# The last part of w_out: row by row through all six gated rows, instead of the first two rows begun on five of them

## What is computed

```
def swiglu(x, w_in, w_out):
    a, b = jnp.split(x @ w_in, 2, axis=-1)
    return (jax.nn.silu(a) * b) @ w_out
...
    for l in range(DEPTH):
        h = h + 0.5 * swiglu(rmsnorm(h, ffn1_norm[l]), ffn1_w_in[l], ffn1_w_out[l])
        u = rmsnorm(h, mix_norm[l])
        ...
        y_c = mem_attention(q_c, rmsnorm(mem, mem_norm[l]), w_mem_kv[l])
        ...
        h = h + 0.5 * swiglu(rmsnorm(h, ffn2_norm[l]), ffn2_w_in[l], ffn2_w_out[l])
    return rmsnorm(h, final_norm)
```

## Time and profile before

| | us |
|---|---|
| median of 3 runs | 2153.34 (2151.99 to 2153.64) |
| the profiled execution | 2153.76 |
| its span in the trace | 2151.7 |
| TensorE busy | 2109.1 (98% of the span) |
| VectorE busy | 1605.8 (75%) |
| GpSimd busy | 1483.6 (69%) |
| ScalarE busy | 1112.0 (52%) |
| chain that ended last: TensorE, VectorE, ScalarE | 92%, 4%, 2% |

### The profile page before, as it was taken

The page is one execution under the profiler, slowest core; times in us unless marked ns, Lnnn a source line. Parts: engine busy times, 40 slices in busy tenths (PEclk is TensorE's granted clock), DMA queues, the critical chain, the costliest instruction groups (busy, mean ns, idle before and its releaser), DMA issues.

```text
span 2151.7 us, 39307 instructions
## 1 busy us (share of the span) xinstructions
PE 2109.1 (98%) x13990; PEld 1917.8 (89%) x13990; DVE 1605.8 (75%) x2860; ACT 1112.0 (52%) x2203; POOL 1483.6 (69%) x1110
## 2 busy tenths in 40 slices
PE   9999998999999999999999999989999999999997
PEld 6999996878888889999889999978888888999996
DVE  6888887468764578888768888765787555888884
ACT  5656653454553356565356565435445533656652
POOL 6888876644445678787778888765444366888874
PEclk9999999999999999999999999999999999999999
DMA  5333333322222323333334333332222133233332
GB/s 171 115 119 103 113 117 113 109 69 69 66 63 85 105 86 105 111 99 105 103 94 133 101 102 125 113 125 85 69 66 73 55 104 97 90 108 99 115 98 83
DMA packets 95234, 213.16 MB, mean 99 GB/s; under 512 B 10401, under 2 KB 13641, under 8 KB 94793
## 3 DMA queue, kind: packets, MB, share of 16 engines
q1 hardware_dynamic: 90864, 205.42, 30.5%
q10 hardware_dynamic: 4184, 5.31, 0.7%
HBM read 208.58 MB, written 3.68 MB: 99 GB/s over the span
## 4 chain that ended last, share of the span: by engine, by line
PE 92%; DVE 4%; ACT 2%; issue 1%; DMA 0%; ACTq 0%; DVEq 0%; SPq 0%
PE banks_two L1082 9%; PE banks_two L1083 9%; PE banks_two L1084 9%; PE bank L1084 7%; PE bank L1083 7%; PE bank L1082 7%; PE bank L950 6%; PE bank L951 6%; PE bank L952 6%; PE banks_two L950 5%; PE banks_two L951 4%; PE banks_two L952 4%; PE tbank L1315 1%; DVE yL L2193 1%; PE bank L1146 1%
## 5 line engine op out<-in xcount | busy, mean ns | idle before, releaser
L806 POOL TENSOR_SCALAR wH<-raw 128x1024 fp32r<-128x1024 f32 (+2 forms) x184 | 173.4, 942 | 416.6 <-PE bank L952 211.2
L809 POOL TENSOR_TENSOR wL<-raw,wH 128x1024 fp32r<-128x1024 f32 (+2 forms) x184 | 389.3, 2116 | 15.4
L851 POOL TENSOR_TENSOR wL<-wS,wH 128x512 fp32r<-128x512 f32 x208 | 268.9, 1301 | 41.9 <-ACT wH L1531 38.4
L851 POOL TENSOR_TENSOR wL<-raw,wH 128x512 fp32r<-128x512 f32 x208 | 267.3, 1301 | 11.6 <-ACT wH L1537 8.0
L1082 PE MATMUL banks_two<-u1H,wH 128*128 128x256 f32 x864 | 244.9, 283 | 3.4 <-DVE far4L L2073 3.4
L1083 PE MATMUL banks_two<-u1H,wL 128*128 128x256 f32 x864 | 244.5, 283 | 0.0
L1084 PE MATMUL banks_two<-u1L,wH 128*128 128x256 f32 x864 | 244.5, 283 | 0.0
L1537 ACT ACTIVATE wH<-raw 128x512 fp32r<-128x512 f32 x208 | 130.5, 630 | 181.1 <-PE bank L1084 181.1
L857 POOL TENSOR_TENSOR wS<-raw 128x512 f32<-128x512 f32 x104 | 135.1, 1299 | 82.7 <-issue 60.6
L950 PE MATMUL bank<-u1H,wH 128*128 128x512 f32 x480 | 191.1, 398 | 0.0
L951 PE MATMUL bank<-u1H,wL 128*128 128x512 f32 x480 | 187.5, 391 | 0.0
(11 more groups left out here) (413 smaller groups left out, 7190.2 us busy)
## 6 DMA issues: line engine op xcount, KB each, us to landing
raw<-in_wA SPq DMA_DIRECT2D x296, 256.0 KB, 3.0
raw<-in_wM SPq DMA_DIRECT2D x96, 512.0 KB, 3.5
raw<-in_wO SPq DMA_DIRECT2D x128, 256.0 KB, 2.9
raw<-in_wA SPq DMA_DIRECT2D x28, 512.0 KB, 3.5
raw<-in_wC SPq DMA_DIRECT2D x32, 384.0 KB, 3.0
raw<-in_wR SPq DMA_DIRECT2D x32, 256.0 KB, 2.6
keep<-in_memT SPq DMA_DIRECT2D x4, 512.0 KB, 5.2
mem<-in_memT SPq DMA_DIRECT2D x2, 1024.0 KB, 5.8
```

What stands on the lines that cost most here:

```text
L806: pool.tensor_scalar(wH[:, w, 0:cols], raw[:, slot, 0:cols], 1.0, 0.0, ALU.mult, ALU.add).then_inc(rounded, 1)
L809: pool.tensor_tensor(wL[:, w, 0:cols], raw[:, slot, 0:cols], wH[:, w, 0:cols].bitcast(F32), ALU.subtract).then_inc(split_done, 1)
L851: pool.tensor_tensor(half_slot(wL_flat, n), full, half_slot(wH_flat, n).bitcast(F32), ALU.subtract).then_inc(pool_low, 1)
```

## The change

Rows 0 and 1 are treated as rows 2 to 7: each output row runs over all six gated rows in turn, and then the next begins. No instruction is added or removed.

```
                             take_unit(u + i)
-                            if i < 2:
-                                rows(i, range(N_OUT - 1))
-                            else:
-                                rows(i, range(N_OUT)).then_inc(unit_used, 1)
-                            if i == 1:
-                                for first in range(2):
-                                    rows(first, (N_OUT - 1,)).then_inc(unit_used, 1)
+                            rows(i, range(N_OUT)).then_inc(unit_used, 1)
```

## The result

| | before | after |
|---|---|---|
| median of 5 runs, us | 2153.34 (2151.99 to 2153.64) | 2163.24 (2160.99 to 2164.11) |
| ratio, 95% interval | | 1.0045 (1.0031 to 1.0060) |
| profiled execution / span | 2153.76 / 2151.7 | 2161.78 / 2159.8 |

The change makes the kernel 9.9 us slower. The forecast was 4.6 slower, and 2163.24 lies above its range.

What follows compares the result with a forecast made beforehand. TensorE, busy 98% of the span, was taken to bound the kernel. Part 2 adds 2 x 2.25 and part 1 2 x 0.05, 4.6 us on the median of 2153.34: 2157.9 us, range 2155.6 to 2160.6.

Steps and rivals of the forecast that it cites:

- The new wait: Row 0's last gated row, both parts and layers: TensorE stands still about 2.15 us, 2.25 with the restart.
- Part 2 reaches the end whole: Feed-forward part 2 of each layer: the 2.25 us delay goes fully to the end, 4.5 us for both.
- Where it is covered: part 1 of each layer: Before the memory projection: VectorE's chain sets its start, so the standstill costs only 0.05 us per layer.
- 9.12 us for the memory's low parts: Part 1, VectorE's chain between output rows 3 and 4: 9.12 us listed for making the memory's low parts.
- isn't waited for in either case: Part 2: GpSimd gets row 0's slot earlier and row 1's later, and nothing waits for it.
- TensorE's own delay of about 2 us shortens its standstill of 7.49 to some 5.5: Memory projection after part 1: TensorE arrives about 2 us later, so its wait falls from 7.49 to some 5.5 us.
- I leave the clock at full: TensorE at the new 2.15 us standstills: no clock fall, as an earlier fall took about 4 us.
- the rival: TensorE's clock falls in all four new standstills, 1.5 us each, row 1 also later: 10.6 us, 2163.9; 4%.
- Both slow rivals: Part 1 not covered, all four standstills count: 9.0 us, 2162.3, 6%; clock falls in the standstills: 10.6, 2163.9, 4%.
- Row 0 handed over sooner: VectorE begins row 0 some 1.1 us sooner in part 1; finishing it earlier brings nothing in part 2.

Runs made afterwards that it cites:

- filled: The change plus nine unread matmuls in each of the four standstills, against the kernel before: 2161.65 us, 1.0040.
- held kernels: Five kernels, old, new or mixed row order, where GpSimd delays weight splits until VectorE's subtractions finish: 2140.21, 2149.77, 2148.01, 2140.35, 2139.51 us against some 2153 before.
- part 2 alone: Row by row order only in feed-forward part 2 of both layers, against the kernel before: 2160.99 us, 1.0036.
- part 1 alone: Row by row order only in feed-forward part 1 of both layers, against the kernel before: 2157.82 us, 1.0020.
- after held: The change, with GpSimd's splits from the third memory slot on waiting for VectorE's subtractions, against the kernel before: 2149.77 us, 0.9983.
- after held earlier: The change, with GpSimd's splits from the second memory slot on waiting for VectorE's subtractions, against the kernel before: 2148.01 us, 0.9977.
- part 2 filled: Row by row order only in feed-forward part 2, nine unread matmuls in each standstill, against the kernel before: 2157.72 us, 1.0021.
- n = 3: Row 1 runs over three gated rows before row 0's last, against before: 2153.13 us; with GpSimd's splits delayed from third or second slot: 2140.35, 2139.51.

## Why the prediction was wrong

**The new wait: right.** All four standstills are 2.15 us with 0.1 for the restart, 2.25 together.

**Part 2 reaches the end whole: right.** 2.26 to 2.3 in each layer where the clock holds (after, filled twice), against 2.25 forecast.

**"Where it is covered: part 1 of each layer": wrong, and this step is the main miss.** It followed VectorE and ScalarE from the copy of row 1 to the copy of row 4 and took the "9.12 us for the memory's low parts" of the earlier trace rows as a fixed length in that chain. It is no length of work. Eight subtractions take 3.25 us. The remaining 6 are waits for GpSimd, and GpSimd's last split in that stretch is released by TensorE's output row 7. So TensorE's order, shut out of the chain by the forecast, comes back into it by GpSimd: 1.5 us in each layer instead of 0.05. The held kernels show it from the other side: with all the splits kept off, the same new order starts the memory projection 0.05 and 0.04 us later. The page of the Trainium skill cited above, "SBUF — State Buffer", section "SBUF: two separate sides", has the rule, and the earlier trace rows had the sign: 9.12 / 8 = 1.14 us for 256 columns, where VectorE's other passes take 0.7 for 512. Of GpSimd the forecast said only, where it treats part 2, that it "isn't waited for in either case"; no semaphore makes VectorE's subtractions wait for a split, and the wait is there all the same.

The sentence "TensorE's own delay of about 2 us shortens its standstill of 7.49 to some 5.5" fell with that step: both ends of the standstill moved, the first by 1.71 and the second by 1.49, and it became 7.26.

**"I leave the clock at full": partly wrong.** The earlier trace rows showed a fall about 4 us after the last matmul, and I took 2.15 as too short. Of the profiled standstills of 2.15 us (after 4, part 2 alone 2, part 1 alone 2, after held 4, after held earlier 4) the clock fell behind 7 of 16, at a price of about 1.65 us (3.91 - 2.26). Where the standstill was filled or covered by nine matmuls it fell at none of 18 places (filled 4, part 2 filled 2, n = 3 in three kernels 12), so the falls are the standstills'. Price and consequence in part 1 were as the rival put them (1.5 each, adding up there too: with a fall +3.13 and +3.08 to the projection in part 1 alone, without one +1.49); its chance of 4% was much too low, and it was put as all or none. The step that failed is to take the 4 us of one fall inside a long standstill as the least that a fall needs.

**The account.** 2 x 2.25 in part 2, 2 x 1.49 in part 1, and for the clock 7/16 x 4 x 1.6 = 2.8: together 10.3, measured 9.9. The share of falls comes from five profiles, so the 2.8 is an estimate. Both slow rivals came true, the one by another path and at a smaller price than its 2.25, the other in part; the forecast gave chances to each but none to both together.

**Row 0 handed over sooner: right.** VectorE begins it 1.1 us sooner, and it brings next to nothing.

Open: what decides whether the clock falls behind a 2.15 us standstill.

## What to carry to other kernels

Before a long VectorE row of many equal passes is taken as work, divide it by their number and compare it with a pass of that shape elsewhere; if it is stretched, look at what GpSimd does there and what releases that. A delay of one engine can come back into another's chain without a semaphore between them. And where an order costs a dependency its cover, n matmuls of other rows over the wait give back just their own length: here nine of the fifteen were enough.

## What the runs showed of the hardware

- VectorE's `scalar_tensor_tensor` of 128x256 with two SBUF inputs takes 0.47 us alone and up to 2.61 beside a GpSimd pass of 2.4 us; each ends 0.28 us behind the GpSimd instruction that it met and that had begun first. Where the subtraction had begun first, GpSimd's pass waited: L806 took 1.29 us instead of 1.05, in both layers of the kernel before. Holding back GpSimd's splits for the length of eight subtractions, twice in an execution, made the kernel 12.9 us faster, more than any change of order did.
- TensorE's clock can go to 1.2 GHz behind a standstill of only 2.15 us. All seven such falls came after work had begun again: 0.45 us behind the restart in part 1 alone (a share of 0.30 at half rate makes the 0.85 of 327 to 328), 0.7 in the kernel after, 1.5 in layer 1 part 1 of the kernel after held. Each lasted about 3.4 us and cost 1.6. The length alone does not decide it. In the filled kernel, early in layer 0's first feed-forward part, it fell behind a shorter standstill too, with 1.80 us of idle time (a share of 0.22 at half rate makes the 0.89). It did so in one of thirteen profiles. Of the ten waits with 2.4 us of idle time in the five kernels that hold GpSimd, four had a fall close by, and one of those began 0.24 us ahead of the restart. The row and the microsecond of the filled kernel:

```profile
63.31 0.39 PE L1082 MATMUL banks_two<-u1H,wH 128*128 128x256 f32 x1 [1.80 <-DVE far4L L2073]
```
```profile
64.00:65.00 1.00, 1.00 (x10) 1.00 (x9) 0.97 (x3) 0.23 (x1) 1.00 (x2) 0.89 0.00 0
```

- The restart behind a wait for VectorE's `far4L` is 0.05 to 0.06 us after that pass's end, and the second matmul comes another 0.11 late, at all of these places alike.
